# Attention heads with the scores one head ahead, and a changed opening, in a two-block transformer layer kernel

## The chip, the core and the metric

The kernel runs on one core of a Trainium2 chip. The metric is the device time of one execution in microseconds. All data is float32. A core has five engines that work side by side and meet only at semaphores: TensorE (PE) multiplies matrices, VectorE (DVE), ScalarE (ACT) and GpSimd (POOL) do element work, SyncE (SP) issues DMA. Each engine takes its instructions strictly in the order in which they are written. So an instruction that waits also holds up everything behind it on its engine.

## The reference, cut to what matters

The input is 256 tokens of width 2048. The first block is sparse attention with a convolution branch, then a gated feed-forward layer. A second block with two other attention branches and another feed-forward layer follows; the change does not touch it. For each of the 16 query heads of the first block three branches are computed and summed with gates:

```python
s_cmp = q @ k_cmp    # 15 compressed keys, made by a small two-layer network from the keys
s_sel = q @ k_slc    # selected blocks; with 256 tokens all causal blocks are selected
s_win = q @ k_win    # window, here all causal keys
p = masked_softmax(s + bias)         # for each branch
out = g0 * (p_cmp @ v_cmp) + g1 * (p_sel @ v_sel) + g2 * (p_win @ v_win)
x = x + concatenate([attn, conv]) @ w_out
```

The convolution branch is a gated linear unit, a causal depthwise convolution with 31 taps, a layer norm over 1024 channels, and `silu`.

## The kernel before, in words

**Weights.** Weights are split in two parts so that the products keep float32 accuracy. A weight *unit* (128 partitions by up to 1152 numbers) is loaded by SP into one of four slots of `w_raw` (`unit`, line 366). ACT writes its high part to `w_hi` (`hi`, line 506). DVE or POOL subtracts and writes the low part to `w_lo` (`lo`, lines 775 and 765). PE multiplies both (`unit`, lines 1333 and 1334). A slot is loaded again when its low part is written, and the high part of a later unit is written when PE has used the unit four before it. In the phases `conv`, `kv`, `gates` and `q` POOL makes all low parts; afterwards DVE makes them.

**Opening.** PE transposes the input; ACT squares it; PE sums the squares; DVE makes the inverse root (`refine`, line 827) and scales the tokens in four groups, each of which ACT copies to a high part and DVE turns into a low part (`norm`, lines 550 and 835). ACT makes the high parts of weight units 0 and 1 before, and those of units 2 and 3 between the first groups. Then ACT issues twelve DMAs with the weights of the compressed branch (lines 584 to 590), which PE first needs after the second group of `kv`, and only then the high part of unit 4. PE multiplies units 0 to 3 (channel group t = 0), then unit 4 and so on.

**Heads.** After the `q` phase a loop over the 16 heads runs on three engines. For a head h:

- PE `scores(h)` (line 1474): 12 products into one of three pairs of banks, h modulo 3; it waits until head h-3 has been copied out of that pair.
- DVE `scores(h)` (line 978): adds the bias, writes to the tile `S[h % 3]`, takes maxima.
- ACT `exps(h)` (line 615): exponentials with their sums.
- DVE `weighted(h)` (line 997): multiplies by gate over sum.
- PE `turns(h)` (line 1488): 8 transposes into the pair of banks of h.
- ACT `turned(h)` (line 623): three copies out of these banks.
- PE `values(h)` (line 1499): 12 products into bank 1. After each second head ACT (`y_hi`) and DVE (`y_lo`) split bank 1 into the operand of the output projection, and the next pair of heads waits for that.

Beside the heads runs the layer norm of the convolution branch (PE sums over `conv_y` in h = 0 and over `conv_sq` in h = 1; DVE centres in h = 0, scales in h = 3, multiplies by the sigmoid in h = 4, makes the low part in h = 5). From h = 6 (`UNIT0`) on, each pass of the loop also holds one unit of the convolution's part of the output projection (`conv_unit(h - 6)`, line 1517). Units 0 to 10 all write bank 0, so that a unit waits until DVE's `conv_out` (line 1015) has added the one before to the residual. The six last units stand behind the loop.

In the order before, PE goes through a pass as `scores(h)`, `conv_unit(h-6)`, `turns(h-1)`, `values(h-1)`. DVE goes through `scores(h)`, `y_lo`, `weighted(h-1)`, low part of unit h-3, `conv_out(h-7)`. ACT goes through `y_hi`, `exps(h)`, `turned(h-1)`, high part of unit h-2.

Of the kernel before, what the change touches and what calls it, by code (L numbers as in the profile page):

```python
# [198 lines left out]
def program(nc, A, cst_d, out):  # L199
# [5 lines left out]
    with ctx:  # L205
# [156 lines left out]
        def _(sp):  # L362
# [33 lines left out]
            for t in range(CT):  # L396
                for u in range(4):
                    unit("conv", 0, 4 * t + u, [(lambda s, h=h: w_raw[:, s, 0:4 * GC].rearrange(
                        "p (k n) -> p k n", n=GC)[:, :, h * P:(h + 1) * P],
                        rows(w_in, 4 * u, 4, ds(CONV0 + h * CCH + t * P, P))) for h in range(2)])  # L400
            for g in range(6):
                for u in range(4):
                    halves("kv", 0, 4 * g + u, w_in, 4 * u, 4, KV0 + g * GC)
# [74 lines left out]
        def _(act):  # L478
# [71 lines left out]
            def norm(k, between=None):  # L550

                if k == 3:
                    x_squares("x_normed", 2)
                root(ROOT[k])
                for b in range(4):
                    act.wait_ge(sem("normed"), 4 * NSPLIT[k] + b + 1)
                    nc.scalar.activation(hp[:, 4 * b:4 * b + 4, 0:T], nrm[:, 4 * b:4 * b + 4, :], ACT.Copy)\
                        .then_inc(sem("normed_hi"), 1)
                    if between and b < 2:
                        between(b)  # L560

# [14 lines left out]
            def his(ph, i, j0, j1):  # L576
                for j in range(j0, j1):
                    hi(ph, i, j)

            x_squares("x_transposed", 1)  # L580
            his("conv", 0, 0, 2)
            norm(0, lambda b: hi("conv", 0, 2 + b))

            act.wait_ge(sem("normed_lo"), 4)
            for half in range(2):
                lo, hi_ = half * HD, (half + 1) * HD
                for kv, w1 in enumerate((w1k, w1v)):
                    act.dma_start(w1[lo:hi_], A["cmp_w1"][0, kv].rearrange("(l d) j -> d l j", d=HD)).then_inc(loaded["cmp"], 16)
                    act.dma_start(pos_rows[0:CLEN, kv, half, :], A["cmp_pos"][0, kv]).then_inc(loaded["cmp"], 16)
                    act.dma_start(w2[lo:hi_, kv, :], A["cmp_w2"][0, kv]).then_inc(loaded["cmp"], 16)  # L590
            def glu_sigmoid(t):
# [44 lines left out]
            for h in range(NQ):  # L636
                if h >= 3 and h % 2:
                    y_hi((h - 3) // 2)
                exps(h)
# [3 lines left out]
                if h == 2:  # L643
                    root(ROOT["conv"], nv_conv)
                if h >= 1:
                    turned(h - 1)
# [6 lines left out]
                if h >= UNIT0:  # L653
                    hi("w_out_conv", 0, h - UNIT0 + 4)
            his("w_out_conv", 0, 14, 16)
            turned(NQ - 1)
            y_hi(NQ // 2 - 1)
            first("w_out")
            stream("w_out", post=squares("w_out"))
# [90 lines left out]
        def _(pool):  # L750
# [9 lines left out]
            for ph in ("conv", "kv", "gates", "q"):  # L760
                for j in range(UPS[ph]):
                    s = slot_of(ph, j)[0]
# [7 lines left out]
        def _(dve):  # L770
# [100 lines left out]
            v.tensor_tensor(small[:, 8:9], vcol("lambda_q1_2"), vcol("lambda_k1_2"), ALU.mult)  # L871
            link(v.tensor_tensor(small[:, 9:10], vcol("lambda_q2_2"), vcol("lambda_k2_2"), ALU.mult))
            norm(0)
            dve.wait_ge(sem("normed_lo"), 4)
# [147 lines left out]
            for h in range(NQ):  # L1022
                scores(h)
                if h >= 3 and h % 2:
                    y_lo((h - 3) // 2)
                if h == 0:
# [24 lines left out]
                if h >= UNIT0 + 1:  # L1051
                    lo("w_out_conv", 0, h - UNIT0 + 3)
                    conv_out(h - UNIT0 - 1)
            lo("w_out_conv", 0, 13)
            conv_out(9)
            lo("w_out_conv", 0, 14)
            weighted(NQ - 1)
            conv_out(10)
            lo("w_out_conv", 0, 15)
            for n in range(11, 14):  # L1060
                conv_out(n)
            y_lo(7)
            first("w_out")
# [251 lines left out]
        def _(pe):  # L1315
# [213 lines left out]
            pe.wait_ge(sem("cmp_kv"), 1)  # L1529
            pe.wait_ge(sem("gates_tok"), 1)  # L1530
            for h in range(NQ):
                scores(h)
                if h == 0:
                    pe.wait_ge(sem("conv_done"), 1)
                    sums(banks[:, 0, 0:T], conv_y, CT).then_inc(sem("conv_sum"), 1)
                if h >= UNIT0:
                    conv_unit(h - UNIT0)
                if h >= 1:
                    turns(h - 1)
                    values(h - 1)  # L1540
                if h == 1:
                    pe.wait_ge(sem("conv_squares"), 1)
                    sums(banks[:, 0, T:], conv_sq, CT).then_inc(sem("conv_sum"), 1)
            for n in range(10, 13):
                conv_unit(n)
            turns(NQ - 1)
            conv_unit(13)
            values(NQ - 1)
            conv_unit(14)
# [174 lines left out]
```

## Time and profile before

| | |
|---|---|
| median of 3 runs | 3314.16 us (3299.47 to 3318.31) |
| the profiled execution's own time, its span | 3313.78 us, 3312.0 us |
| PE busy, share of the span | 3002.6 us, 91% |
| DVE busy | 2118.6 us, 64% |
| ACT busy | 1297.0 us, 39% |
| POOL busy | 180.1 us, 5% |
| granted clock of PE, mean over the span | 0.957 |
| DMA | 507.25 MB, mean 153 GB/s |

The span is what the trace covers; the execution's own time is 1.8 us more. The granted clock is a share of TensorE's full 2.4 GHz; 0.50 is 1.2 GHz. A busy share is a mean over very different stages. Those that the change touches are the opening (the first 65 us) and the heads (some 285 to 565 us).

### The profile page before, as it was taken

The numbers are of one execution on the slowest core, as the hardware profiler recorded it, in microseconds if no ns is written. First come the engines' busy times: TensorE is split into PE (matmuls) and PEld (weight loads), VectorE is DVE, ScalarE is ACT, GpSimd is POOL, SyncE is SP. The second block draws the span as 40 slices with busy tenths as digits, with TensorE's granted clock in tenths as the row PEclk, the third lists the DMA queues.
The fourth block names the chain that finished last, engine by engine and source line by source line (L and its number), as shares of the span: only waits on it lengthen the run. The fifth ranks groups of instructions, "written<-read, shape, count | busy, mean of one in ns | idle before, by whom it ended". The sixth has DMA issues, their size and how long they took to land.

```text
span 3312.0 us, 49487 instructions
## 1 busy us (share of the span) xinstructions
PE 3002.6 (91%) x16768; PEld 2570.6 (78%) x16768; DVE 2118.6 (64%) x3212; ACT 1297.0 (39%) x1613; POOL 180.1 (5%) x84
## 2 busy tenths in 40 slices
PE   6998557899999999977999998988998999999998
PEld 5886346788888888866778777777887888888887
DVE  3965434688578668656776565655765665665665
ACT  3323323444333333333444344444434443343333
POOL 4862000000000000000000000000000000000000
PEclk8998678999999999988999999999998999999999
DMA  7653013555555555533545454544554655555653
GB/s 198 178 146 90 13 32 76 141 177 178 192 171 189 183 178 173 176 109 91 144 144 164 154 159 133 152 147 138 185 187 129 190 184 187 187 182 186 189 170 122
DMA packets 595859, 507.25 MB, mean 153 GB/s; under 512 B 90027, under 2 KB 594619, under 8 KB 595131
## 3 DMA queue, kind: packets, MB, share of 16 engines
q1 hardware_dynamic: 585408, 501.42, 49.3%
q10 hardware_dynamic: 9803, 2.59, 0.4%
q0 software_dynamic: 560, 2.12, 0.2%
q8 instruction: 49, 0.80, 0.1%
q14 instruction: 39, 0.32, 0.0%
HBM read 503.88 MB, written 2.12 MB: 153 GB/s over the span
## 4 chain that ended last, share of the span: by engine, by line
PE 79%; DVE 14%; issue 3%; ACT 2%; ACTq 1%; DVEq 0%; DMA 0%; POOL 0%
PE banks L1333 48%; PE banks L1334 24%; DVE w_lo L780 3%; DVE arena L796 2%; PE banks L1376 1%; PE banks L1320 1%; ACT w_hi L512 1%; DVE arena L1099 1%; DVE arena L843 1%; PE banks L1368 1%; DVE hp_f L1006 1%; DVE hp_f L990 1%; PE banks L1482 1%; DVE arena L1127 0%; DVE yp L1131 0%
## 5 line engine op out<-in xcount | busy, mean ns | idle before, releaser
L1333 PE MATMUL banks<-hp,w_hi 128*128 128x512 f32 x5120 | 1842.1, 403 | 122.8 <-DVE w_lo L780 67.1
L512 ACT ACTIVATE w_hi<-w_raw 128x1024 fp32r<-128x1024 f32 (+2 forms) x960 | 991.7, 1045 | 1299.7 <-PE banks L1334 1125.1
L1334 PE MATMUL banks<-hp,w_lo 128*128 128x256 f32 x5120 | 1445.4, 282 | 0.0
L780 DVE TENSOR_TENSOR w_lo<-w_raw,w_hi 128x1024 fp32r<-128x1024 f32 (+2 forms) x886 | 1047.1, 1205 | 566.0 <-ACT w_hi L512 546.3
L1333 PEld LDWEIGHTS banks<-hp,w_hi 128*128 128x128 f32 x5120 | 973.4, 190 | 377.8 <-issue 79.3
L1334 PEld LDWEIGHTS banks<-hp,w_lo 128*128 128x128 f32 x5120 | 978.7, 191 | 2.1 <-issue 1.7
L1333 PE MATMUL banks<-yp,w_hi 128*128 128x512 f32 x2176 | 789.1, 406 | 63.5 <-DVE x L1020 56.5
L1334 PE MATMUL banks<-yp,w_lo 128*128 128x256 f32 x2176 | 619.3, 285 | 0.0
L1333 PEld LDWEIGHTS banks<-yp,w_hi 128*128 128x128 f32 x2176 | 418.5, 192 | 168.0 <-DVE x L1020 57.6
L1334 PEld LDWEIGHTS banks<-yp,w_lo 128*128 128x128 f32 x2176 | 420.9, 193 | 0.1
L796 DVE TENSOR_REDUCE arena<-banks 128x256 f32<-128x512 f32 (+1 forms) x392 | 251.1, 682 | 198.1 <-PE banks L1334 197.8
L765 POOL TENSOR_TENSOR w_lo<-w_raw,w_hi 128x1024 fp32r<-128x1024 f32 x74 | 177.9, 2408 | 78.4 <-ACT w_hi L512 78.4
L1333 PE MATMUL banks<-arena_r,w_hi 128*128 128x512 f32 x272 | 100.9, 410 | 14.7 <-DVE w_lo L780 14.4
L990 DVE SCALAR_TENSOR_TENSOR hp_f<-banks,arena 128x512 f32<-128x512 f32 (+1 forms) x64 | 18.8, 357 | 140.6 <-PE banks L1486 140.5
L897 DVE SCALAR_TENSOR_TENSOR banks<-arena,vec,banks 128x256 f32<-128x256 f32 x232 | 102.0, 485 | 3.6
L669 ACT ACTIVATE arena<-arena 128x512 f32<-128x512 f32 x44 | 27.8, 632 | 158.3 <-DVE arena L1099 110.1
L1099 DVE SCALAR_TENSOR_TENSOR arena<-arena,vec 128x256 f32<-128x256 f32 x176 | 77.5, 481 | 12.8 <-DVE arena L1093 5.8
L1334 PE MATMUL banks<-arena_r,w_lo 128*128 128x256 f32 x272 | 77.5, 285 | 0.0
L1333 PEld LDWEIGHTS banks<-arena_r,w_hi 128*128 128x128 f32 x272 | 52.4, 193 | 28.6 <-issue 14.5
L620 ACT ACTIVATE hp_f<-hp_f,small 128x7 f32<-128x7 f32 (+2 forms) x96 | 37.5, 391 | 82.4 <-DVE small L995 82.4
L1376 PE MATMUL banks<-arena,cst 128*128 128x256 f32 x192 | 47.8, 402 | 18.8 <-ACT arena L572 12.3
L1071 DVE TENSOR_TENSOR x<-banks,x 128x256 f32 (+1 forms) x128 | 53.1, 415 | 17.5 <-PE banks L1334 17.5
(198 smaller groups left out, 1456.7 us busy)
## 6 DMA issues: line engine op xcount, KB each, us to landing
w_raw<-in_w_in SPq DMA_DIRECT2D x480, 256.0 KB, 3.2
w_raw<-in_w_up SPq DMA_DIRECT2D x352, 256.0 KB, 3.6
w_raw<-in_w_ffn_up SPq DMA_DIRECT2D x176, 256.0 KB, 3.4
w_raw<-in_w_ffn_gate SPq DMA_DIRECT2D x176, 256.0 KB, 3.0
w_raw<-in_w_down SPq DMA_DIRECT2D x160, 256.0 KB, 2.9
w_raw<-in_w_ffn_down SPq DMA_DIRECT2D x160, 256.0 KB, 2.9
w_raw<-in_w_out SPq DMA_DIRECT2D x128, 256.0 KB, 3.1
w_raw<-in_w_mla_proj SPq DMA_DIRECT2D x64, 256.0 KB, 2.9
```

Source lines behind the costliest of these rows:

```text
L512: nc.scalar.activation(w_hi[:, s, 0:n], w_raw[:, s, 0:n], ACT.Copy).then_inc(hi_ready, 1)
L620: ins = nc.scalar.activation(e[:, lo:hi_], e[:, lo:hi_], ACT.Exp, bias=m[:, j:j + 1], accum_out=l[:, j:j + 1])
L765: nc.gpsimd.tensor_tensor(w_lo[:, s, 0:n], w_raw[:, s, 0:n], w_hi[:, s, 0:n].bitcast(f32), ALU.subtract)\
L780: v.tensor_tensor(w_lo[:, s, 0:n], w_raw[:, s, 0:n], w_hi[:, s, 0:n].bitcast(f32), ALU.subtract)\
L796: v.tensor_reduce(dst, pair(b)[0:rows], X, ALU.add).then_inc(chunk_out, 1)
L897: ins = v.scalar_tensor_tensor(conv_y[:, t, :] if k == TAPS - 1 else acc, src, w, acc, ALU.mult, ALU.add)
L990: ins = v.scalar_tensor_tensor(dst, src, HD ** -0.5, b, ALU.mult, ALU.add)
L1071: link(v.tensor_tensor(xt, banks[:, c, 0:T], xt, ALU.add))
L1099: ins = v.scalar_tensor_tensor(dst[:, c, :], buf[:, c, k:k + T], vdyn("ffn_conv_w", at_ch[c] + k * 2 * FT), dst[:, c, :], ALU.mult, ALU.add)
L1333: mm(banks[:, b, :], w_hi[:, s, at:at + P], rhs[:, kt, :], start=kt == kt_first, stop=False)
L1334: ins = mm(banks[:, b, 0:T], w_lo[:, s, at:at + P], rhs[:, kt, 0:T], start=False, stop=kt == kt_last)
L1376: ins = mm(banks[:, 4, 0:T], ones, sq[:, t, :], start=t == 0, stop=t == KT - 1)
```

## The change

1. SP issues the twelve DMAs of the compressed branch, between its weight units 3 and 4; ACT no longer does.
2. ACT makes the high parts of units 0, 1 and 2 ahead of the norm, and that of unit 3 between the root and the first copy.
3. DVE makes the low parts of units 0, 1 and 2 ahead of its norm; POOL starts with unit 3.
4. PE goes through a pass of the head loop as `scores(h+1)`, `turns(h-1)`, `conv_unit(h-6)`, `values(h-1)`, with `scores(0)` ahead of the loop. The sums over `conv_sq` stand between `turns(0)` and `values(0)`.
5. DVE goes through `scores(h)`, `conv_out(h-7)`, steps of the layer norm, `weighted(h-1)`, low part of unit h-3, `y_lo`. ACT goes through `exps(h)`, `y_hi`, `turned(h-1)`, high part of unit h-2.
6. Behind the loop the last head's transposes come first, then unit 10, its value products, and units 11 to 15.

```diff
@@ SP, opening
+                if t == 0:
+                    for half in range(2):
+                        lo, hi_ = half * HD, (half + 1) * HD
+                        for kv, w1 in enumerate((w1k, w1v)):
+                            sp.dma_start(w1[lo:hi_], ...).then_inc(loaded["cmp"], 16)
+                            sp.dma_start(pos_rows[0:CLEN, kv, half, :], ...).then_inc(loaded["cmp"], 16)
+                            sp.dma_start(w2[lo:hi_, kv, :], ...).then_inc(loaded["cmp"], 16)
@@ ACT, opening
                 root(ROOT[k])
+                if between:
+                    between()
                 for b in range(4):
...
-                    if between and b < 2:
-                        between(b)
...
-            his("conv", 0, 0, 2)
-            norm(0, lambda b: hi("conv", 0, 2 + b))
-            act.wait_ge(sem("normed_lo"), 4)
-            for half in range(2):
...
+            his("conv", 0, 0, 3)
+            norm(0, lambda: hi("conv", 0, 3))
@@ ACT, heads
-                if h >= 3 and h % 2:
-                    y_hi((h - 3) // 2)
                 exps(h)
...
+                if h >= 3 and h % 2:
+                    y_hi((h - 3) // 2)
                 if h >= 1:
                     turned(h - 1)
...
-            his("w_out_conv", 0, 14, 16)
             turned(NQ - 1)
+            hi("w_out_conv", 0, 14)
             y_hi(NQ // 2 - 1)
+            hi("w_out_conv", 0, 15)
@@ POOL
-                for j in range(UPS[ph]):
+                for j in range(3 if ph == "conv" else 0, UPS[ph]):
@@ DVE, opening
+            lows("conv", 0, 0, 3)
             norm(0)
@@ DVE, heads
                 scores(h)
-                if h >= 3 and h % 2:
-                    y_lo((h - 3) // 2)
+                if h >= UNIT0 + 1:
+                    conv_out(h - UNIT0 - 1)
...
                     lo("w_out_conv", 0, h - UNIT0 + 3)
-                    conv_out(h - UNIT0 - 1)
+                if h >= 3 and h % 2:
+                    y_lo((h - 3) // 2)
+            conv_out(9)
+            weighted(NQ - 1)
             lo("w_out_conv", 0, 13)
-            conv_out(9)
+            conv_out(10)
             lo("w_out_conv", 0, 14)
-            weighted(NQ - 1)
-            conv_out(10)
+            y_lo(7)
             lo("w_out_conv", 0, 15)
...
@@ PE, heads
+            scores(0)
+            pe.wait_ge(sem("conv_done"), 1)
+            sums(banks[:, 0, 0:T], conv_y, CT).then_inc(sem("conv_sum"), 1)
             for h in range(NQ):
-                scores(h)
...
+                if h < NQ - 1:
+                    scores(h + 1)
+                if h >= 1:
+                    turns(h - 1)
+                if h == 1:
+                    pe.wait_ge(sem("conv_squares"), 1)
+                    sums(banks[:, 0, T:], conv_sq, CT).then_inc(sem("conv_sum"), 1)
                 if h >= UNIT0:
                     conv_unit(h - UNIT0)
                 if h >= 1:
-                    turns(h - 1)
                     values(h - 1)
...
-            for n in range(10, 13):
+            turns(NQ - 1)
+            conv_unit(10)
+            values(NQ - 1)
+            for n in range(11, 14):
                 conv_unit(n)
-            turns(NQ - 1)
-            conv_unit(13)
-            values(NQ - 1)
             conv_unit(14)
             conv_unit(15)
```

## Rows read from the trace of the kernel before

**Rows 1.** The page's chain that ended last, by engine and line.

```profile
PE 79%; DVE 14%; issue 3%; ACT 2%; ACTq 1%; DVEq 0%; DMA 0%; POOL 0%
```

**Rows 2.** Stretches: length, each engine's busy time (instructions), PE clock, DMA share, GB/s.

```profile
285.00:559.00 274.00, 164.14 (x767) 129.64 (x768) 112.92 (x336) 84.09 (x269) 0.00 (x0) 0.74 0.11 31
364.00:368.00 4.00, 4.00 (x15) 3.28 (x13) 0.00 (x0) 0.38 (x1) 0.00 (x0) 0.50 0.00 0
379.00:391.00 12.00, 9.74 (x61) 7.87 (x60) 3.87 (x16) 4.88 (x17) 0.00 (x0) 1.00 0.00 0
474.00:491.00 17.00, 9.80 (x50) 7.96 (x49) 5.77 (x19) 4.52 (x17) 0.00 (x0) 0.80 0.11 31
```

**Rows 3.** Waits, 285 to 580 us: us in total, times, longest.

```profile
DVE hp_f L990 <- PE banks L1486: 140.5, 14, 13.3
PE banks L1333 <- DVE x L1020: 56.5, 10, 6.3
```

**Rows 4.** The chain: end of head 5, then one pass: start us, us, what.

```profile
389.40 0.63 PE banks L1482 x2
...
443.36 1.19 DVE hp_f L990 x4
446.06 1.27 DVE hp_f L1006 x6
449.31 0.80 PE banks L1333
454.32 0.89 PE banks L1320 x8
456.40 0.65 PE banks L1508 x2
458.49 0.63 PE banks L1482 x2
460.38 1.19 DVE hp_f L990 x4
```

**Rows 5.** PE in time: head 2, head 3 at the low clock, units 10 to 14.

```profile
348.02 1.12 PE L1508 MATMUL banks<-hp_f,arena 128*64 128x256 f32 x2 [1.20 <-ACT hp_f L629]
357.54 1.97 PE L1320 MATMUL banks<-cst,hp_f 128*128 128x128 f32 x8 [4.07 <-DVE hp_f L1006]
360.71 1.11 PE L1508 MATMUL banks<-hp_f,arena 128*64 128x256 f32 x2 [1.20 <-ACT hp_f L629]
364.50 1.22 PE L1482 MATMUL banks<-arena 64*128 64x256 f32 x2
544.93 0.50 PE L1333 MATMUL banks<-yp,w_hi 128*128 128x512 f32 x1 [0.91 <-DVE x L1020]
553.51 1.03 PE L1320 MATMUL banks<-cst,hp_f 128*128 128x128 f32 x8
559.28 0.50 PE L1333 MATMUL banks<-yp,w_hi 128*128 128x512 f32 x1
```

**Rows 6.** DVE in time, head 3: from the layer norm's first step to the weights.

```profile
335.02 1.74 DVE L830 RECIPROCAL hp_f<-hp_f 128x256 f32<-128x256 f32 x1
343.09 0.18 DVE L1002 RECIPROCAL small<-small 128x6 f32<-128x6 f32 x1
```

**Rows 7.** All engines in time, opening.

```profile
31.03 3.25 DVE L843 SCALAR_TENSOR_TENSOR arena<-x,vec,arena 128x256 f32<-128x256 f32 x8
34.82 5.35 POOL L765 TENSOR_TENSOR w_lo<-w_raw,w_hi 128x1024 fp32r<-128x1024 f32 x2 [8.84 <-ACT w_hi L512]
35.34 5.90 DVE L843 SCALAR_TENSOR_TENSOR arena<-x,vec,arena 128x256 f32<-128x256 f32 x4
57.56 3.90 ACT L512 ACTIVATE w_hi<-w_raw 128x1024 fp32r<-128x1024 f32 x4 [12.51 <-issue]
61.19 0.77 PE L1333 MATMUL banks<-hp,w_hi 128*128 128x512 f32 x1 [9.16 <-POOL w_lo L765]
```

**Rows 8.** DMA queues, 54 to 56 us: packets, MB, share.

```profile
q10 hardware_dynamic: 1640, 0.41, 121.6%
```

More of the change, by code:

```diff
@@ L400, in _ @@
                         rows(w_in, 4 * u, 4, ds(CONV0 + h * CCH + t * P, P))) for h in range(2)])
+                if t == 0:
+                    for half in range(2):
+                        lo, hi_ = half * HD, (half + 1) * HD
+                        for kv, w1 in enumerate((w1k, w1v)):
+                            sp.dma_start(w1[lo:hi_], A["cmp_w1"][0, kv].rearrange("(l d) j -> d l j", d=HD)).then_inc(loaded["cmp"], 16)
+                            sp.dma_start(pos_rows[0:CLEN, kv, half, :], A["cmp_pos"][0, kv]).then_inc(loaded["cmp"], 16)
+                            sp.dma_start(w2[lo:hi_, kv, :], A["cmp_w2"][0, kv]).then_inc(loaded["cmp"], 16)
             for g in range(6):
@@ L580, in _ @@
             x_squares("x_transposed", 1)
-            his("conv", 0, 0, 2)
-            norm(0, lambda b: hi("conv", 0, 2 + b))
-            act.wait_ge(sem("normed_lo"), 4)
-            for half in range(2):
[L586 to L590, printed above, removed]
+            his("conv", 0, 0, 3)
+            norm(0, lambda: hi("conv", 0, 3))
             def glu_sigmoid(t):
@@ L1061, in _ @@
                 conv_out(n)
-            y_lo(7)
             first("w_out")
@@ L1530, in _ @@
             pe.wait_ge(sem("gates_tok"), 1)
+            scores(0)
+            pe.wait_ge(sem("conv_done"), 1)
+            sums(banks[:, 0, 0:T], conv_y, CT).then_inc(sem("conv_sum"), 1)
             for h in range(NQ):
-                scores(h)
-                if h == 0:
-                    pe.wait_ge(sem("conv_done"), 1)
-                    sums(banks[:, 0, 0:T], conv_y, CT).then_inc(sem("conv_sum"), 1)
+                if h < NQ - 1:
[5 more added lines that the diff above has]
+                    sums(banks[:, 0, T:], conv_sq, CT).then_inc(sem("conv_sum"), 1)
                 if h >= UNIT0:
@@ L1538, in _ @@
                 if h >= 1:
-                    turns(h - 1)
                     values(h - 1)
-                if h == 1:
-                    pe.wait_ge(sem("conv_squares"), 1)
-                    sums(banks[:, 0, T:], conv_sq, CT).then_inc(sem("conv_sum"), 1)
-            for n in range(10, 13):
+            turns(NQ - 1)
+            conv_unit(10)
+            values(NQ - 1)
+            for n in range(11, 14):
                 conv_unit(n)
-            turns(NQ - 1)
-            conv_unit(13)
-            values(NQ - 1)
             conv_unit(14)
```

## The prediction

> **What bounds the kernel now.** I read the page's chain first: 79% of the end time is PE's own work and 14% DVE's [rows 1]. So a gain has to come from places where PE stands still or runs slow. The table of stretches shows where that is. In the head stage, 285 to 559 us, PE is busy for 164 of 274 us at a mean granted clock of 0.74, while DVE (113 us) and ACT (84 us) have still more room [rows 2]. No engine bounds this stage; a ring of waits does. The waits name it: DVE's score step waits 140.5 us for PE's score products, and PE's projection units wait 56.5 us for DVE's addition to the residual [rows 3]. They wait for each other in turn.
>
> The chain of one pass shows the ring in order [rows 4]. DVE starts at 443.36, finishes the weights at 446.06 + 1.27 = 447.3 and the addition at 449.3. PE then runs the unit to 454.3, the transposes, waits for ACT's copies, runs the value products from 456.4 and the scores of the next head from 458.5 to 460.38, when DVE starts again. Nothing overlaps: 5.95 (DVE) + 5.01 (unit) + 2.08 (transposes and copies) + 2.09 (values) + 1.89 (scores) = 17.02 us. The unit is slow for a second reason. PE comes to it from 6 us of idleness, at 1.2 GHz. Three units in a row behind a short wait took 553.51 - 544.93 = 8.58 us [rows 5], 2.86 each.
>
> The opening has one large hole: PE waits 9.16 us at 61.19 for POOL's low part of unit 4 [rows 7]. ACT spent 12.51 us before 57.56 mostly on issuing DMAs and made that unit's high part only then.
>
> **The passes from h = 7 to 15 (edits 4 and 5).** PE's work per pass stays the same, but `scores(h+1)` stands ahead of the transposes, so DVE finds the scores of its next head ready. At the full clock PE needs 1.89 (scores) + 0.89 (transposes) + 2.09 (values) [rows 4] + 2.86 (unit) [rows 5] = 7.73 us. I count the others from the end of unit h-7, as 0:
>
> - PE: `values(h-2)` to 2.1, `scores(h+1)` to 4.0, `turns(h-1)` to 4.9, `conv_unit(h-6)` to 7.7.
> - DVE: `conv_out(h-7)`, the stretch of two additions, to 0.9; `weighted(h-1)` some 1.7 more, to 2.6, which is 1.4 before PE wants it; a low part (1.2) and half the time `y_lo` (0.4), to 4.2; `scores(h+1)` with its maxima (443.36 to some 445.7, 2.3) to 6.5. Then it waits for the unit. In all 5.8 to 6.2 us of work, the 5.77 us of a pass [rows 2].
> - ACT: a high part to 1.1, `exps(h)` (2.4) to 3.5, the copies of h-1 from 4.9 to 6.1, before PE wants them at 7.7. In all some 4.5 us [rows 2].
>
> So PE is the bound with 1.4 us to spare at the closest place, and as it then hardly stops I take the full clock. What is queued behind `conv_out`, which now waits for the unit ahead of `weighted`, is `weighted(h-1)` and through it `turns(h-1)`; that is the 1.4 us. In the last pass there are no scores to fill the time, so it takes 6.5 us. From the end of `values(5)` to the end of `values(14)` the kernel before took 389.4 [rows 4] to 543.9 (1 us ahead of unit 10 [rows 5]), 154.5 us for nine passes, 17.2 each. After: 8 x 7.7 + 6.5 = 68.1. Gain 86.4 us.
>
> **The passes h = 0 to 6.** In the kernel before's own time: nothing moves up to `turns(0)`, 303.0 to 305.0, since DVE is then the later one; `scores(1)` and `scores(2)` run in PE's idle time. The sums over `conv_sq` take 5.4 (310.4), `values(0)`, `scores(3)`, `turns(1)` 2.1 + 1.9 + 0.9 (315.3), copies 1.2, `values(1)`, `scores(4)` to 320.4. DVE has the scores of head 3 at 314.3, does them to 316.6, then the norm block, 343.09 - 335.02 = 8.1 us [rows 6], and the weights of head 2 to 326.4. `turns(2)` runs at the low clock, 2.0, and after the copies `values(2)` starts at 329.6, where before it started at 348.0 [rows 5]. The same walk through the sigmoid (table load and 1.9 us on ACT) and the two long DVE steps of h = 4 and 5 brings `turns(3)` to 335, `turns(4)` to 341.5, unit 0 to 348.5 and the end of `values(5)` to 353.4, against 389.4. Gain 36.0 us. This is the least certain term: at the low clock a head takes 1.97 (transposes), 3.79 (values) [rows 5] and 3.6 (scores) where it takes 4.9 at full, so I bound it by 28 and 40.
>
> **Behind the loop (edit 6).** `turns(15)` waits for `weighted(15)`, 0.7 us; unit 10, the values and units 11 to 13 follow at 2.86 each with their low parts ready. Unit 14 starts at 436.5 against 559.28 [rows 5]. That is 122.8, so this part brings 0.4; bounds -1 and +2.
>
> **The opening (edits 1 to 3).** Before, PE ends its first four units and a bias product at 52.0 and starts unit 4 at 61.19. After, ACT is free for unit 4's high part when unit 0 has been used and the token copies are done, at some 43 to 45 us, and POOL needs 2.4 us more: ready at 48. Unit 4 starts at 51.9, gain 9.2. It also no longer starts at the low clock; before, five pairs of products took 0.64 each against 0.355, another 1.4. Units 5 to 7 follow every 2.8 us, and POOL makes a low part in 2.4.
>
> The twelve DMAs on SP cost 10.8 us of issue (most of the 12.51 that ACT spent [rows 7]), from some 6 to 17 us, while SP waits for slots anyway. Their data stand in SP's queue ahead of units 4 to 7. By the DMA view that queue ran dry at some 20 us; the compressed weights' 256-byte packets went at 1640 in 2 us [rows 8], so 8192 of them take 10 us, the bias table's 5.5 us beside them and the weight units 5: unit 4 lands at some 37 and unit 7 at some 43, against 43 to 51 where they are wanted. Cost nothing; if that cover is gone, PE starts unit 4 as much later.
>
> The low parts on DVE (3 x 1.2 us) lie between 21 and 25 us, where DVE waits for the sum of squares until 26.96. POOL no longer runs beside the scaling: before, four scalings took 5.90 us beside POOL's two low parts, while eight took 3.25 alone [rows 7]. That frees 4.3 us. But POOL's low part of unit 3 now falls at 29 to 31.4, on the refinement, which is two-operand DVE work as well, for up to 2.4 us. PE starts unit 0 between 35.5 and 37.3, runs it slowly for 5.1 as before, and finds unit 1 ready at 40.6 to 42.4, against 42.42. Gain 0 to 1.9; I take 0.1, since the scalings beside POOL were held for all but the gaps.
>
> The Trainium skill (SBUF — State Buffer, SBUF: two separate sides) says that VectorE and GpSimd hold a shared pair of ports for a whole instruction and the other one blocks. By that rule the low part of unit 3 blocks the refinement whole, which gives the 0.1; a kinder reading of the row would give 1.9. The trace agrees with the rule: 1.48 us for each scaling beside POOL against 0.41.
>
> **Sum.** 86.4 + 36.0 + 0.4 + 9.2 + 1.4 + 0.1 = 133.5 us. The profiled execution took 3313.8 us, practically the runs' median (3314.2), so 3180.3. I forecast 3181.
>
> **Rivals.**
>
> *A. The clock stays low in the passes.* For: in heads 1 to 4 it falls to 0.50 after each wait and stays there a while, even over 4 us of full work [rows 2]. Against: from 379 to 391 us it is 1.00 with transposes, copies waited for and products alternating [rows 2]. Price: a pass is then 5.01 + 1.97 + 3.79 + 3.6 = 14.4 us, 6.7 more; nine of them 60, so 3241. Chance 0.06. The Trainium skill (TensorE: Matmul & The Clock Gate, Part 4: PE-mode transpose) says that transposes do not count as busy the way matmuls do; by that rule the passes would run at 1.2 GHz for part of the time, up to this 3241. The row at 379 us speaks against it, as only 0.9 us of a pass is transposes.
>
> *B. DVE becomes the bound.* If it comes late to the scores, their 2.3 us and a low part fall into the ring of unit, `conv_out`, `weighted`, transposes: 2.9 + 0.9 + 1.7 + 0.9 + 2.3 + 1.2 = 9.8 us a pass, 2.1 more, nine times 19: 3200. It decides once the hand-overs cost the 1.4 us I have to spare. Chance 0.10.
>
> *C. The scores do not get ahead*, since they still need a bank pair free of head h-2. They would then stand where they stood, and only the opening's 10.7 us come: 3303. Against: the copies of h-2 end some 1.5 us before the unit of the pass before ends. Chance 0.02.
>
> *D. The opening brings nothing*, since the loads on SP's queue come late for unit 4 by as much as ACT's did: 3191. Chance 0.04.
>
> *E. Slower.* The clock stays low and DVE's block does not overlap: PE's 14.4 us and DVE's 5.95 in line are 20.3 us a pass against 17.2, nine times 3.1 = 28 us more, less 10.7 of the opening: 3331. It decides where DVE gets the scores of a head only in the pass in which it has to weigh it. Chance 0.02.
>
> **How the numbers follow.** My case, 3166 to 3198 by its bounds (the early passes 28 to 40, the opening 1.9, the passes 7.6 to 8.5), has 0.76. With B and D the range 3166 to 3205 holds 0.8 or more. This kernel tells 0.5% (16 us) from no change. Faster by more: all but C and E, 0.96; within: C, 0.02; slower: E, 0.02.
>
> **What would show it.** Right: DVE's score step waiting little for PE's line 1486, PE's wait for line 1020 gone, passes 7.7 us apart at clock 1.00, unit 4 of the opening near 52 us without a 9 us wait. Wrong: a clock of 0.5 to 0.8 in the passes (A), PE's transposes waiting for line 1006 in each pass (B), or a wait for a DMA at unit 4 (D). The rest of the trace should be the same, only earlier.

## The result, and the profile after

| | before | after |
|---|---|---|
| median | 3311.76 us (4 runs, 3299.47 to 3318.31) | 3184.87 us (4 runs, 3164.55 to 3193.52) |
| profiled execution, its span | 3313.78, 3312.0 us | 3188.14, 3186.3 us |
| granted clock, mean | 0.957 | 0.970 |

The ratio is 0.9612, with an interval of 0.9557 to 0.9667. So the kernel is faster by 3.3 to 4.4%, and 3184.87 lies 4 us above the forecast 3181. The profiled executions differ by 125.6 us, where the sum said 133.5. The four times after lie 29 us apart, so that a distance of 4 us to the forecast is partly luck. The last stage of this kernel can run at two paces (experiment 12); both profiled executions had the slower one, so the 125.6 us hold nothing of that.

From the page of the kernel after: the engines' busy time with their instructions, and the chain by engine. PE's share of the chain is 81%, against 79% [rows 1].

```profile
PE 2977.2 (93%) x16768; PEld 2553.2 (80%) x16768; DVE 2121.1 (67%) x3215; ACT 1296.4 (41%) x1613; POOL 172.6 (5%) x81
...
PE 81%; DVE 12%; issue 3%; ACT 2%; DVEq 0%; ACTq 0%; DMA 0%
```

To see where the 125.6 us came from, I cut both traces at the same milestones of PE's order. The times are starts of the first instruction of a step, or ends of the last:

| stretch | before | after | gain | forecast |
|---|---|---|---|---|
| start to `scores(0)` | 285.9 | 271.9 | 14.0 | 10.7 |
| `scores(0)` to the end of `values(5)` | 103.4 | 78.8 | 24.6 | 36.0 |
| to the end of `values(14)` | 154.6 | 67.8 | 86.8 | 86.4 |
| to unit 14 | 15.3 | 15.0 | 0.3 | 0.4 |

The waits of the head stage, 270 to 440 us, after: total, times, longest. They answer to [rows 3].

```profile
ACT hp_f L627 <- PE banks L1323: 40.1, 15, 8.0
ACT w_hi L519 <- PE banks L1337: 32.1, 17, 3.0
DVE x L1021 <- PE banks L1337: 21.1, 12, 3.5
DVE hp_f L992 <- PE banks L1489: 12.7, 8, 6.5
...
PE banks L1323 <- DVE hp_f L1008: 11.8, 4, 6.0
```

DVE waited 140.5 us for scores and now waits 12.7. PE's wait for the addition to the residual (56.5 us) is gone. The waits that are left belong to ACT and DVE, which are not the bound. PE itself waits for DVE's weights four times, and the longest of these, 6.0 us, is in head 2.

Two stretches after, in the columns of [rows 2]: the early heads, and the passes with units.

```profile
304.00:344.00 40.00, 30.41 (x113) 23.05 (x112) 26.25 (x76) 18.34 (x57) 0.00 (x0) 0.53 0.05 14
344.00:411.00 67.00, 67.00 (x409) 54.72 (x407) 50.21 (x164) 38.99 (x136) 0.00 (x0) 0.98 0.22 64
```

In the passes PE is busy in 67.00 of 67 us at a clock of 0.98. Before it was busy for 9.80 of 17 us at 0.80 [rows 2]. The 0.98 holds the slow first products of unit 0, up to 347 us; from 360 to 406 us the clock is 1.00. The early heads read quite otherwise: a clock of 0.53 over 40 us. That is where the forecast lost its 11 us.

One pass after, PE and DVE in time (start, length, engine, line; in brackets idle time and what ended it). It answers to [rows 4]:

```profile
356.33 0.65 PE L1511 MATMUL banks<-hp_f,arena 128*64 128x256 f32 x2
358.35 0.70 PE L1485 MATMUL banks<-arena 64*128 64x256 f32 x2
360.20 1.09 PE L1323 MATMUL banks<-cst,hp_f 128*128 128x128 f32 x8
363.99 0.65 PE L1511 MATMUL banks<-hp_f,arena 128*64 128x256 f32 x2
...
356.43 0.42 DVE L1021 TENSOR_TENSOR x<-banks,x 128x256 f32<-128x256 f32 x1 [1.23 <-PE banks L1337]
357.65 1.28 DVE L1008 TENSOR_SCALAR hp_f<-hp_f,small 128x7 f32<-128x7 f32 x6
360.30 1.18 DVE L992 SCALAR_TENSOR_TENSOR hp_f<-banks,arena 128x512 f32<-128x512 f32 x4 [0.24 <-PE banks L1489]
```

Value products at 356.33, scores at 358.35, transposes at 360.20, the unit, and value products again at 363.99: a period of 7.66 us, in which PE's rows carry no bracket. DVE ends the weights at 357.65 + 1.28 = 358.93, and PE wants them at 360.20. The slack is 1.27 us.

### The profile page after: what moved, and what is told of

Its sections match the earlier page's. It is cut to its first block, busy times and chain, and to the rows that moved or that the text cites. A ratio compares the mean times of both kernels' runs of the same rounds, so it can differ in the third digit from the quotient of the medians.

```text
span 3186.3 us, 49487 instructions
## 1 busy us (share of the span) xinstructions
PE 2977.2 (93%) x16768; PEld 2553.2 (80%) x16768; DVE 2121.1 (67%) x3215; ACT 1296.4 (41%) x1613; POOL 172.6 (5%) x81
## 4 chain that ended last, share of the span: by engine, by line
PE 81%; DVE 12%; issue 3%; ACT 2%; DVEq 0%; ACTq 0%; DMA 0%
PE banks L1336 49%; PE banks L1337 25%; DVE w_lo L781 3%; DVE arena L797 2%; PE banks L1379 1%; PE banks L1323 1%; ACT w_hi L519 1%; DVE arena L1102 1%; PE banks L1371 1%; DVE arena L1130 1%; DVE yp L1134 1%; DVE arena L844 1%; DVE arena L1131 1%; PE banks L1485 0%; ACT arena L670 0%
## 5 line engine op out<-in xcount | busy, mean ns | idle before, releaser
L1336 PE MATMUL banks<-yp,w_hi 128*128 128x512 f32 x2176 | 771.3, 399 | 6.6 <-DVE yp L1134 5.3
L1337 PE MATMUL banks<-yp,w_lo 128*128 128x256 f32 x2176 | 610.8, 281 | 0.0
L1336 PEld LDWEIGHTS banks<-yp,w_hi 128*128 128x128 f32 x2176 | 410.1, 188 | 107.5 <-DVE yp L1134 6.6
L1337 PEld LDWEIGHTS banks<-yp,w_lo 128*128 128x128 f32 x2176 | 412.1, 189 | 0.1
L766 POOL TENSOR_TENSOR w_lo<-w_raw,w_hi 128x1024 fp32r<-128x1024 f32 x71 | 170.4, 2402 | 71.9 <-ACT w_hi L519 71.9
L1336 PEld LDWEIGHTS banks<-arena_r,w_hi 128*128 128x128 f32 x272 | 52.4, 193 | 28.7 <-issue 14.5
L1379 PEld LDWEIGHTS banks<-arena,cst 128*128 128x128 f32 x192 | 38.5, 207 | 27.8 <-ACT arena L579 14.9
L704 ACT ACTIVATE arena<-arena,small 128x128 f32<-128x128 f32 x64 | 28.6, 448 | 74.1 <-DVE small L1182 74.1
```

Of the source, the lines that this page charges most:

```text
L766: nc.gpsimd.tensor_tensor(w_lo[:, s, 0:n], w_raw[:, s, 0:n], w_hi[:, s, 0:n].bitcast(f32), ALU.subtract)\
L1336: mm(banks[:, b, :], w_hi[:, s, at:at + P], rhs[:, kt, :], start=kt == kt_first, stop=False)
L1337: ins = mm(banks[:, b, 0:T], w_lo[:, s, at:at + P], rhs[:, kt, 0:T], start=False, stop=kt == kt_last)
L1379: ins = mm(banks[:, 4, 0:T], ones, sq[:, t, :], start=t == 0, stop=t == KT - 1)
```

## Experiments

There were twelve runs, of ten new kernels; experiment 11 is the kernel after once more and experiment 12 that of experiment 7. Where a total and a stage of the trace disagree I read the stage. One kernel's executions lie up to 29 us apart (after: 3164.55 to 3193.52), and a single total tells no difference under that.

**1. The heads alone.** The kernel before with edits 4, 5 and 6.

> The kernel before with the changed order of the heads alone (edits 4 to 6), opening as before. Theory (a ring of waits in the heads, independent of the opening): the profiles of before and after differ by 111.6 us from the first scores on, so 3313.8 - 111.6 = 3202 us, between 3190 and 3212, passes of the head loop 7.7 us. Rival (the heads profit from an opening that ends earlier or otherwise, so the parts do not add up): over 3215.

Measured: 3201.82 us, ratio to before 0.9676 (0.9647 to 0.9706). `scores(0)` starts at 285.91, as before (285.94), DVE waits for scores 12.7 us, as after, and the passes are 7.7 us apart. The medians differ by 100.4 us, and the ratio makes it 107 of the 3302.25 that before took on that chip. In the traces the part from `scores(0)` on shrank from 3026.1 to 2916.9 us, by 109.2, where before and after differ by 111.6. The theory holds in the stage. That the total hit 3202 was partly luck: it had been counted from 3313.8, and before took 11.6 less here.

**2. The opening alone.** The kernel before with edits 1, 2 and 3.

> The kernel before with the changed opening alone (edits 1 to 3). Theory: first scores of the heads at 272 us in place of 286, total 3300 us, 3293 to 3304. Rival (the opening's gain is given back at the heads, where DVE or the loads are late): not under 3309.

Measured: 3290.51 us, ratio 0.9966 (0.9945 to 0.9987), 4 to 18 us less than before. That is under the expected 3293 to 3304, which again had been counted from 3313.8; the stage is as expected. `scores(0)` starts at 272.98, 13.0 us earlier. DVE's wait for scores is 141.7 us, as in the kernel before. The two halves add up: 0.9676 x 0.9966 = 0.9643, against 0.9612 measured for both, within the intervals; 10 us are left open by them.

**3. PE's old order in the loop.** The kernel after; DVE and ACT keep the new order, and so does what stands behind the loop.

```diff
             for h in range(NQ):
-                if h < NQ - 1:
-                    scores(h + 1)
+                if h:
+                    scores(h)
+                if h >= UNIT0:
+                    conv_unit(h - UNIT0)
                 if h >= 1:
                     turns(h - 1)
+                    values(h - 1)
...
-                if h >= UNIT0:
-                    conv_unit(h - UNIT0)
-                if h >= 1:
-                    values(h - 1)
```

> The changed kernel, but PE keeps the old order inside the head loop (scores of this pass, unit, transposes, values); DVE and ACT keep their new order. Theory: both orders are links of one ring. DVE's addition now comes 3.2 us after the scores (2.3 + 0.9) in place of 5.95, the weights lie beside the unit; a pass is 3.2 + 4.7 (unit) + 2.1 + 2.1 + 1.9 = 14.0 us, 6.3 more than 7.7, nine times 57, and some 20 more in heads 1 to 5: 3262 us, 3245 to 3275. Rival (the order on DVE and ACT does nothing without PE's): passes of 17 us, 3188 + 86 + 25 = 3299.

Measured: 3257.89 us. The passes are 13.7 to 14.5 us apart (transposes at 370.23, 384.75, 398.84, 412.73, 426.53, 440.25). Both waits of the ring are back: DVE's for scores, and PE's for the addition. The rows are from this kernel in time, DVE's wait of one pass and PE's wait of another:

```profile
390.96 1.18 DVE L992 SCALAR_TENSOR_TENSOR hp_f<-banks,arena 128x512 f32<-128x512 f32 x4 [8.22 <-PE banks L1489]
...
379.71 0.79 PE L1336 MATMUL banks<-yp,w_hi 128*128 128x512 f32 x1 [3.25 <-DVE x L1022]
```

The new order of DVE and ACT alone takes a pass from 17.2 to some 14; the rest, down to 7.7, needs PE's.

**4. PE's new order, with the old one on DVE and ACT.**

```diff
@@ ACT
+                if h >= 3 and h % 2:
+                    y_hi((h - 3) // 2)
                 exps(h)
...
-                if h >= 3 and h % 2:
-                    y_hi((h - 3) // 2)
@@ DVE
                 scores(h)
-                if h >= UNIT0 + 1:
-                    conv_out(h - UNIT0 - 1)
+                if h >= 3 and h % 2:
+                    y_lo((h - 3) // 2)
...
                     lo("w_out_conv", 0, h - UNIT0 + 3)
-                if h >= 3 and h % 2:
-                    y_lo((h - 3) // 2)
+                    conv_out(h - UNIT0 - 1)
```

> The changed kernel, but DVE and ACT keep their old order inside the head loop; PE has the new one. Theory: PE's order carries nearly all; on odd passes DVE waits for the split of bank 1 ahead of the weights and PE for the addition, 1.8 us, on even ones nothing: passes of 9.5 and 7.7 in turn, 8 us more in all than the changed kernel, 3196 us, 3188 to 3202. Rival (DVE's order carries a large part, as the addition stands behind the weights and a low part in each pass): 10 us or more each pass, over 3209.

Measured: 3209.82 us. That is above the 3188 to 3202 of the theory. The total just reaches the rival's 3209, but its passes of 10 us or more are not there: they are 8.8 and 8.4 us in turn, with one of 11.3 and one of 10.1 among the nine. So both missed. I had put the price on `conv_out`, which runs late; from 280 to 580 us PE waits for it 3.1 us in all. The trace puts the price on `y_lo`. A wait of this kernel (270 to 440 us), and one instance with the weights behind it:

```profile
DVE yp L1014 <- ACT yp L634: 29.1, 7, 6.3
```

```profile
373.80 0.42 DVE L1014 TENSOR_TENSOR yp<-banks,yp 128x256 fp32r<-128x256 f32 x1 [3.87 <-ACT yp L634]
...
374.56 1.28 DVE L1008 TENSOR_SCALAR hp_f<-hp_f,small 128x7 f32<-128x7 f32 x6
```

`y_hi` on ACT and `y_lo` on DVE need the value products, which now stand last in PE's pass. Where they stand ahead of `exps` and `weighted`, both engines sit still until PE has ended its pass, 3.87 us here, and the weights come late. So moving `y_hi` and `y_lo` back is a needed part of edit 5, and PE's order is most of the gain: a pass of 17.2 becomes 8.4 to 8.8 by it alone, 9.0 on average with the two long ones. In the two long ones the granted clock fell to 0.50 (395 to 399 us, and 415 to 417).

**5. Of the opening, the DMAs on SP alone.** The kernel after, without edits 2 and 3: `his("conv", 0, 0, 2)` and `between(b)` as before, POOL from unit 0 on, no `lows` on DVE.

> The changed kernel, but of the opening's edits only the twelve DMAs of the compressed branch on SP; high and low parts of units 0 to 3 as in the kernel before. Theory (ACT's issue time was the hole): unit 4 starts at some 52 us without a long wait and the heads' first scores at 275 us (before 285.9, changed kernel 271.9). Rival (the hole was closed by the low parts on DVE): unit 4 at 58 us or later, first scores over 281 us.

Measured: 3189.22 us. The bias product and the first product of unit 4:

```profile
51.09 1.02 PE L1415 MATMUL banks<-yp_f,cst 128*128 128x512 f32 x2
51.55 0.80 PE L1335 MATMUL banks<-hp,w_hi 128*128 128x512 f32 x1
```

No wait is left at unit 4, and it starts 9.6 us earlier than before (61.19). `scores(0)` starts at 275.25.

**6. Of the opening, the low parts on DVE alone.** The kernel after with the twelve DMAs issued by ACT, behind the norm, as before.

> The changed kernel, but the twelve DMAs stay on ACT, behind the token copies; the low parts of units 0 to 2 on DVE and ACT's order as changed. Theory: the token copies end some 3 us earlier than in the kernel before (43.4 against 46.3), the issue still takes 10.8 us, so unit 4 starts at some 58.2 us and the first scores come at 283 us. Rival (the low parts carry the opening's gain): first scores at 275 us or earlier.

Measured: 3188.81 us; `scores(0)` at 283.95, 2.0 us earlier than before. ACT and PE at unit 4:

```profile
55.21 3.90 ACT L512 ACTIVATE w_hi<-w_raw 128x1024 fp32r<-128x1024 f32 x4 [12.66 <-issue]
...
58.84 0.77 PE L1336 MATMUL banks<-hp,w_hi 128*128 128x512 f32 x1 [7.08 <-POOL w_lo L766]
```

The hole is there as long as ACT issues these DMAs. So of the 14.0 us of the opening some 10.7 belong to edit 1 (experiment 5) and the rest to edits 2 and 3. That rest is 0.9 to 3.4 us, since `scores(0)` moves by 2.5 us between executions with the same opening. Both totals are within 5 us of the kernel after, though the stage is 3 and 12 us longer; the spread named above hides it. In experiment 6 the last stage also ran at the quicker of its two paces, which is worth 13 us (experiment 12).

**8 and 9. More work for DVE in each pass.** Additions to unused numbers, behind `conv_out`: two instructions, then six.

```diff
                 if h >= UNIT0 + 1:
                     conv_out(h - UNIT0 - 1)
+                    for _ in range(2):    # six in the other kernel
+                        v.tensor_tensor(conv_sq[:, _, :], c_("cos"), c_("sin"), ALU.mult)
```

> The changed kernel with two more DVE instructions of 0.42 us in each pass from h = 7 on, between the addition and the weights (they compute nothing that is used). The trace of the changed kernel shows DVE's weights ending 1.27 us ahead of PE's transposes. Theory (PE is the bound): the 0.84 us vanish, passes stay at 7.67 us. Rival (DVE or the hand-overs are the bound): passes of 8.5 us, 8 us more in all.

> The same with six such instructions, 2.5 us in each pass. Theory (PE is the bound with 1.27 us to spare, and then the ring unit, addition, weights, transposes): passes of 7.67 + 2.5 - 1.27 = 8.9 us, some 11 us more in all. Rival (DVE is the bound): 10.2 us, 23 us more. Rival (nothing rings: DVE's whole work of 8.4 us bounds it): 8.4 us.

Measured: 3190.39 and 3194.1 us. With two the passes are 7.7 us apart (352.77, 360.48, 368.15, 375.87). With six they are 8.48 apart. Of that kernel, two transposes in turn, and between them DVE's residual addition with its wait, and its six additions:

```profile
380.51 1.09 PE L1325 MATMUL banks<-cst,hp_f 128*128 128x128 f32 x8 [0.72 <-DVE hp_f L1008]
388.99 1.10 PE L1325 MATMUL banks<-cst,hp_f 128*128 128x128 f32 x8 [0.73 <-DVE hp_f L1008]
...
384.43 0.42 DVE L1021 TENSOR_TENSOR x<-banks,x 128x256 f32<-128x256 f32 x1 [0.55 <-PE banks L1339]
385.23 2.09 DVE L1029 TENSOR_TENSOR hp_f<-cst 128x256 f32<-128x256 f32 x6
```

The six take 2.09 us, not 2.5. The slack of 1.27 swallows the first part: 7.67 + 2.09 - 1.27 = 8.49, and 8.48 is measured. The second rival's 8.4 lies as near, but only because it took 2.5 us for the six: DVE is busy for 39.89 of the 42.44 us of five passes, 7.98 in each, and still waits for the unit ahead of its addition. So it is the ring and not DVE's whole work. PE bounds the pass and DVE is second by 1.27 us, so rival B's mechanism is real and begins just there.

**7. PE kept at work in the early heads.** The changed kernel leaves the early heads at a clock of 0.50. Is this a matter of what PE does, so that unused products in its pauses would lift it?

```diff
+            def fill(n):
+                for _ in range(n):
+                    mm(banks[:, 0, :], ones, cst[:, 0:512], start=True, stop=True)
...
+                if h == 3:
+                    fill(6)
                 if h >= 1:
                     turns(h - 1)
+                if 2 <= h < UNIT0:
+                    fill(1)
```

> The changed kernel with products on PE that nobody reads (128x512, 0.86 us each at the full clock, into bank 0, which is free there): six ahead of the transposes of h = 3, where PE idles 6 us, and one behind the transposes of h = 2 to 5, where it waits 1.2 us for ACT's copies. In the changed kernel's trace the clock is 0.50 from some 307 to 347 us and a pass of h = 4 or 5 takes 10.5 us. Theory (the clock is what the early heads lost against the forecast): the clock stays at 1.00 in them, passes of some 6 to 7 us, unit 0 starts 10 to 13 us earlier and the execution takes 3188 - 11 = 3177 us. Rival (the early heads are bound by DVE's layer norm steps and ACT's tables, not by the clock): under 3 us earlier, or later by the products.

Measured: 3161.07 us (3160.04 to 3170.02), ratio to before 0.9579 (0.9560 to 0.9599). Ahead of `turns(2)`, the added products, the wait that is left, and the longest wait in the heads behind it:

```profile
307.09 5.42 PE L1533 MATMUL banks<-cst 128*128 128x512 f32 x12
313.14 1.09 PE L1323 MATMUL banks<-cst,hp_f 128*128 128x128 f32 x8 [0.64 <-DVE hp_f L1008]
...
323.41 0.65 PE L1511 MATMUL banks<-hp_f,arena 128*64 128x256 f32 x2 [2.15 <-ACT hp_f L629]
```

The same head in the kernel after, and the transposes of the next one, 10.47 us later:

```profile
311.32 1.97 PE L1323 MATMUL banks<-cst,hp_f 128*128 128x128 f32 x8 [5.98 <-DVE hp_f L1008]
314.49 1.11 PE L1511 MATMUL banks<-hp_f,arena 128*64 128x256 f32 x2 [1.21 <-ACT hp_f L629]
...
321.79 1.97 PE L1323 MATMUL banks<-cst,hp_f 128*128 128x128 f32 x8
```

With the 6 us filled the clock stays at 1.00. From `scores(0)` to `turns(5)` it takes 333.45 - 274.18 = 59.3 us, against 342.74 - 271.93 = 70.8 after. The total lies 16 us under the expected 3177, since in this execution the last stage also ran at the quicker of its two paces (experiment 12).

**10. The same with transposes in place of products:** `for _ in range(8 * n): turn(banks[:, 0, 0:P], c_("ones"))`.

> The same filling by transposes of 128x128 in place of products (eight for each product, about as long at the full clock). Theory (the clock follows PE's products and not its transposes): the clock falls as in the changed kernel, the transposes run at the low clock and take twice as long, first unit no earlier than in the changed kernel, 3188 to 3196 us. Rival (any activity holds the clock): as with products, some 3177 us.

Measured: 3176.4 us. The same stretch takes 335.76 - 274.04 = 61.7 us. A window of this kernel that is mostly transposes, and these in time:

```profile
308.00:312.00 4.00, 4.00 (x36) 3.89 (x35) 3.90 (x6) 1.48 (x7) 0.00 (x0) 1.00 0.00 0
```

```profile
309.39 5.46 PE L1323 MATMUL banks<-cst 128*128 128x128 f32 x48
```

48 transposes in a row kept the granted clock at 1.00 just as the products did. So the theory that only products hold it fell, and its rival stands: here transposes hold it too. Whether they could also raise a low clock, no run shows. The Trainium skill (TensorE: Matmul & The Clock Gate, Part 4: PE-mode transpose) has it that transposes don't count as busy in the same way; for these float32 transposes the measurement decides, and it says that they hold the clock as products do.

**11 and 12. The changed kernel and the filled one, side by side**, unaltered, on one chip.

> The changed kernel itself, on the same chip and in the same rounds as the next one, since the comparison of e7 with the earlier runs of the changed kernel mixes the executions' own spread. Theory: 3184 us, 3175 to 3192; passes of h = 4 and 5 at the low clock, 10.5 us, in this execution too. Rival (the low clock there was an accident of one execution): 6 to 7 us.

> The kernel of e7 (products that nobody reads, in the waits of h = 2 to 5) once more. Theory: from the heads' first scores to the transposes of h = 6 it takes 59 us against 71 in the changed kernel, so 12 us less in all: 3172 us, ratio to the changed kernel 0.9962. Rival (the 24 us between the medians of e7 and of the changed kernel are of the filling): 3160 us.

Measured: 3179.66 us (3170.17 to 3181.97), ratio to before 0.9615 (0.9596 to 0.9635), for the changed kernel; 3178.24 us (3162.43 to 3183.29), ratio 0.9601 (0.9575 to 0.9627), for the filled one. The early heads, the changed kernel first and then the filled one:

```profile
304.00:344.00 40.00, 30.41 (x113) 23.06 (x112) 26.25 (x76) 18.32 (x57) 0.00 (x0) 0.53 0.05 14
```

```profile
304.00:344.00 40.00, 36.52 (x201) 25.94 (x200) 34.11 (x102) 24.86 (x76) 0.00 (x0) 1.00 0.09 27
```

The stage is the same as the first time: 342.74 - 272.24 = 70.5 us against 331.32 - 271.84 = 59.5. Yet the medians differ by 1.4 us, and the intervals overlap. The filled kernel's six times are 3162.43, 3163.06, 3177.22, 3179.26, 3182.71 and 3183.29, in two groups at least 14 us apart. The expectation held in the stage; of its totals neither 3172 nor the rival's 3160 came.

The traces show where the 11 us go. This is the first product of the second block's feed-forward layer, the changed kernel first and then the filled one, and then, in the same order, 500 us of that layer:

```profile
2404.39 0.79 PE L1336 MATMUL banks<-hp,w_hi 128*128 128x512 f32 x1 [8.74 <-DVE hp L849]
...
2398.07 0.79 PE L1336 MATMUL banks<-hp,w_hi 128*128 128x512 f32 x1 [8.74 <-DVE hp L849]
```

```profile
2500.00:3000.00 500.00, 500.00 (x2886) 437.28 (x2885) 315.86 (x377) 206.66 (x201) 0.00 (x0) 1.00 0.60 189
...
2500.00:3000.00 500.00, 500.00 (x2832) 433.63 (x2831) 308.52 (x368) 201.28 (x196) 0.00 (x0) 1.00 0.59 186
```

At this layer the filled kernel is still 6.3 us ahead. From there to the end of the span it takes 3175.4 - 2398.1 = 777.3 us, and the changed one 3168.4 - 2404.4 = 764.0. PE is busy without a gap and the granted clock is 1.00 in both, but a pair of products takes 0.3465 us in the changed kernel and 0.353 in the filled one. This is not the filling's doing: the profiled execution of the kernel after has 2832 products in this window, and that of experiment 7, which is filled, 2887. Another 7 us go between the heads and this layer: at `turns(15)` the filled kernel was 13.2 us ahead (405.83 against 419.08). There the traces of one kernel differ by as much as 5 us, too: the kernel after takes 2409.46 - 419.18 = 1990.3 us for this part, in experiment 11 it takes 1985.3, and the two traces of the filled kernel take 1992.2 and 1986.8.

Compared at equal pace, the filled kernel is ahead by 3168.4 - 3159.3 = 9.1 us (experiments 11 and 7) and by 3186.3 - 3175.4 = 10.9 us (the kernel after and experiment 12). So it is shown twice that the early heads lose 11 us to the clock, and in these two pairs of traces most of it arrives at the end. But they are two pairs, from different sets of runs, and the times without a trace can't be sorted by pace. By the times alone no version is shown to beat the changed kernel.

## Why the prediction was right, and where its sum was off

**What bounds the kernel.** Right. The ring of waits [rows 3, 4] was what the head stage cost; experiment 3 brings it back with its two waits.

**The passes h = 7 to 15.** 86.8 us came where 86.4 were forecast. A pass takes 7.67 us (forecast 7.73) at a clock of 1.00. DVE's slack is 1.27 (forecast 1.4), measured twice, in the trace and by experiments 8 and 9. Rival B touched only the last pass, with a wait of 0.56 us (412.67). The tail brought 0.3 of 0.4.

**The passes h = 0 to 6.** The mis-sized term: 36.0 us forecast, with bounds of 28 and 40, and 24.6 measured, outside the bounds. The step that failed is the last of that walk, "brings `turns(3)` to 335, `turns(4)` to 341.5, unit 0 to 348.5 and the end of `values(5)` to 353.4". Counted from `scores(0)`, `turns(3)` was forecast at 49.1 us and came at 321.79 - 271.93 = 49.9. Up to there the walk held in its sum, with `turns(2)` 1.1 us early and the head behind it 10.5 us long where it had 8.6. From there the forecast took 6.5 to 7 us a head, which is the full clock, and the chain of the kernel after shows 10.5 us a head:

```profile
321.86 1.91 PE banks L1323 x8
...
332.34 1.91 PE banks L1323 x8
...
342.81 1.90 PE banks L1323 x8
```

These are 1.97 + 1.2 + 3.8 + 3.5, close to the low-clock durations that the same paragraph lists [rows 5] and then uses for its bound alone; and even that bound, 28, was too high. I took it that the clock would recover once the waits were gone. It didn't, though PE stood still for only 1.20 us in 10.47. It was rival A's mechanism, in the three heads where I had not looked for it, and not in the nine passes where I had; the unit with its long row of products lifts the clock. Experiment 7 shows the size: at a clock of 1.00 the stretch up to `turns(5)` is 11.5 us shorter. Over the term's whole stretch, to the end of `values(5)` and so with unit 0, which also began slowly after, it takes 65.2 us against 78.8. By that the term would have been 38.2, within the bounds and 2 us above the forecast.

**The opening.** 14.0 us where 10.7 were forecast. The hole of 9.16 us is gone; unit 4 starts at 49.90, 2.0 us before the 51.9 forecast. Unit 1 starts at 41.13 in place of 42.42, a gain of 1.3 where I took 0.1: PE no longer waits 1.55 us for the second group of tokens, and the clock rose earlier, after five pairs of products where there had been eight. The hole's slow start is gone as forecast, 1.2 us. That leaves 1.5 us between 52 and 272 us. `scores(0)` started between 271.84 and 274.36 in ten profiled executions with the twelve DMAs, the high and the low parts all moved, so much of this differs from one execution to the next; its cause is open.

"Cost nothing" for the twelve DMAs held, but the path was another. I had SP issue them from 6 to 17 us in 10.8 us, and the load of unit 4 wait behind their data until 37. SP's own rows of the kernel after, two of the twelve and the loads from unit 4 on, and then ACT:

```profile
18.11 4.75 SPq L406 DMA_DIRECT2D arena<-in_cmp_pos  x1
...
24.13 8.24 SPq L406 DMA_DIRECT2D arena<-in_cmp_pos  x1
...
40.45 8.74 SPq L371 DMA_DIRECT2D w_raw<-in_w_in  x10
```

```profile
44.70 1.06 ACT L519 ACTIVATE w_hi<-w_raw 128x1024 fp32r<-128x1024 f32 x1 [2.67 <-DMA w_raw<-in_w_in]
```

SP began with the twelve at 16.78 and was done at 40.41, after 23.6 us. The four of line 406 took 2.0 to 8.2 us each to issue, where the same four had taken 1.4 to 1.5 on ACT. The load of unit 4 was issued only then, at 40.45, and ACT had it at 44.70, 7.7 us after my 37. The DMA engines were nearly full in most of this time, with the bias table's transfer among the rest, but which of these held SP's issue back no run shows. POOL's low part was ready at 48.2, 1.7 us before PE wanted it; a queue slower by these 1.7 us would have cost.

The refinement beside POOL's low part, from the kernel after:

```profile
29.46 1.83 DVE L832 TENSOR_TENSOR arena<-arena 128x256 f32<-128x256 f32 x1
...
36.54 1.67 DVE L844 SCALAR_TENSOR_TENSOR arena<-x,vec,arena 128x256 f32<-128x256 f32 x4
...
28.67 2.33 POOL L766 TENSOR_TENSOR w_lo<-w_raw,w_hi 128x1024 fp32r<-128x1024 f32 x1 [8.10 <-ACT w_hi L519]
```

DVE's step ends at 31.29, 0.3 us behind POOL's, and takes 1.83 us where a step of that size takes 0.42. Four scalings without POOL beside them take 1.67 us, against 5.90 [rows 7]. This is the blocking for a whole instruction that the Trainium skill (SBUF — State Buffer, SBUF: two separate sides) states, and the trace agrees. Unit 0 started at 36.73, 1.2 us later than before, and within the 35.5 to 37.3 I gave.

The two errors, +3.3 in the opening and -11.4 in the early heads, partly cancel; the total was closer than its parts.

## What to carry to other kernels

Where two engines wait for each other in turn, look for the step that one of them could do a round earlier, and then, on every in-order engine, put the instruction whose input comes last at the end of the pass: either half alone left some 1 to 6 us in a pass here. When you forecast such a walk, carry the clock as a state from step to step, and give the low one its own price wherever PE's work is a row of small products broken by waits. When DMAs move to another engine, ask when that engine gets to its next load: here it was 23.6 us later, and the cover left was 1.7 us. An engine that isn't the bound after the change deserves a measured slack: here it was 1.27 us, and 2.09 us of further work already cost 0.8 in each pass.

## What the runs showed of the hardware that was not expected

The clock can stay at 1.2 GHz under a nearly full PE. Windows of the kernel after, two of many:

```profile
316.00:320.00 4.00, 4.00 (x15) 2.96 (x14) 2.91 (x4) 3.97 (x8) 0.00 (x0) 0.50 0.00 0
328.00:332.00 4.00, 4.00 (x16) 3.30 (x14) 1.46 (x2) 1.30 (x6) 0.00 (x0) 0.50 0.00 0
```

PE's records fill these windows, and the granted clock is 0.50 in both. It fell in the pause of 5.98 us ahead of `turns(2)`, and it rose only when the units' long rows of products had begun, some 347 us. With the pause filled by products or by transposes it did not fall at all, over waits of up to 2.15 us. In experiment 4 it fell in a pass with waits of only 0.70 and 0.62 us. What was not tried is which of the added instructions it takes: those in the long pause, or those behind the transposes of each head.

The last feed-forward layer runs at two paces at one granted clock of 1.00. From 2600 to 3000 us PE is busy for all 400 us in each of the fourteen traces; nine of them hold 2265 or 2266 products and five hold 2309 or 2310, whatever the kernel. Over the layer this makes 13 us, more than several of the changes compared here. What sets the pace no trace shows.

Issuing a DMA takes the issuing engine's time, and how much depends on more than the transfer: the same four took 1.4 to 1.5 us each on ACT and 2.0 to 8.2 on SP in the opening. On ACT, twelve of them were most of the 12.66 us in experiment 6.
